# First mixer: X at the head of SyncE's load queue, branch a's convolution started earlier, its norm placed between the output projection's pieces

## The reference, cut to what matters

```
def conv_mixer(x, w_in, a_dw, a_dw_b, a_ln_g, a_ln_b, b_dw, w_out):
    u = jnp.einsum("bsd,de->bse", x, w_in)                       # 1024 -> 2560
    a_val, a_gate, b_b, b_c, b_x = jnp.split(u, [...], axis=-1)   # 512 features each
    a = a_val * jax.nn.sigmoid(a_gate)
    a = causal_depthwise_conv(a, a_dw) + a_dw_b                   # 31 taps
    a = jax.nn.silu(layer_norm(a, a_ln_g, a_ln_b))
    bb = b_b * causal_depthwise_conv(b_c * b_x, b_dw)             # 3 taps
    return jnp.einsum("bse,ed->bsd", jnp.concatenate([a, bb], axis=-1), w_out)
```

## Time and profile before

| | |
|---|---|
| median of 3 runs | 1865.94 us (1864.38 to 1869.52) |
| the profiled execution: its time | 1861.7 us |
| its span, first to last instruction | 1860.4 us |
| mean granted TensorE clock | 0.983 |
| busy TensorE matmul / weight load | 92% / 60% |
| busy VectorE / ScalarE / GpSimd | 43% / 33% / 7% |
| chain that ended last | PE 67%, DMA 21%, DVE 6%, ACT 3% |

### The profile page before, as it was taken

How to read it: one execution, slowest core, us unless ns; L and a number is a source line. 1 busy time by engine, 2 the same in 40 slices (tenths; PEclk the granted TensorE clock), 3 DMA queues, 4 the chain that set the end, 5 groups by cost and what they waited for, 6 DMA issues and landing times.

```text
span 1860.4 us, 23739 instructions
## 1 busy us (share of the span) xinstructions
PE 1710.4 (92%) x9910; PEld 1113.5 (60%) x9910; DVE 796.0 (43%) x1526; ACT 611.4 (33%) x1159; POOL 121.3 (7%) x141
## 2 busy tenths in 40 slices
PE   7978999998887987999998988699999999999998
PEld 7964443333232974344432322587999789779986
DVE  4952111111002774111110010566788667758885
ACT  4531010000001561011000001366666554646664
POOL 0000000000000000000000000033111000501110
PEclk9989999999999999999999999899999999999999
DMA  9439999999999639999999999443455544335550
GB/s 397 181 146 366 420 419 420 420 420 421 419 420 418 231 146 408 421 419 420 420 419 421 420 419 419 157 140 136 155 184 183 181 159 159 133 125 184 182 181 24
DMA packets 75362, 544.87 MB, mean 293 GB/s; under 512 B 8433, under 2 KB 8433, under 8 KB 9457
## 3 DMA queue, kind: packets, MB, share of 16 engines
q1 hardware_dynamic: 74304, 540.05, 73.0%
q10 hardware_dynamic: 944, 3.22, 0.4%
HBM read 542.19 MB, written 1.05 MB: 292 GB/s over the span
## 4 chain that ended last, share of the span: by engine, by line
PE 67%; DMA 21%; DVE 6%; ACT 3%; issue 1%; POOL 1%; SPq 0%; DVEq 0%; ACTq 0%
PE PS L897 21%; DMA ring<-in_w 16%; PE PS L342 12%; PE PS L344 12%; PE PS L343 12%; DMA F<-in_w 5%; PE PS L874 2%; PE PS L909 2%; PE PS L655 1%; DVE wl L325 1%; POOL sm L437 1%; DMA X<-in_x 1%; DVE X L547 1%; ACT wh L319 1%; PE PS L492 0%
## 5 line engine op out<-in xcount | busy, mean ns | idle before, releaser
L897 PE MATMUL PS<-ring,F 128*64 128x512 f32 x2112 | 477.7, 597 | 45.7 <-DMA ring<-in_w 41.3
L325 DVE TENSOR_TENSOR wl<-ring,wh 128x512 fp32r<-128x512 f32 x512 | 367.9, 739 | 187.2 <-ACT wh L319 184.2
L319 ACT ACTIVATE wh<-ring 128x512 fp32r<-128x512 f32 x512 | 319.4, 631 | 295.0 <-PE PS L344 291.4
L897 PEld LDWEIGHTS PS<-ring,F 128*64 128x64 f32 x2112 | 144.1, 136 | 362.7 <-issue 269.1
L342 PE MATMUL PS<-xh,wl 128*128 128x256 f32 x1216 | 351.5, 289 | 6.9 <-DVE xl L1547 2.1
L343 PE MATMUL PS<-xl,wh 128*128 128x256 f32 x1216 | 344.7, 283 | 0.0
L344 PE MATMUL PS<-xh,wh 128*128 128x256 f32 x1216 | 344.6, 283 | 0.0
L342 PEld LDWEIGHTS PS<-xh,wl 128*128 128x128 f32 x1216 | 233.9, 192 | 11.4 <-issue 5.8
L343 PEld LDWEIGHTS PS<-xl,wh 128*128 128x128 f32 x1216 | 234.1, 192 | 0.6
L344 PEld LDWEIGHTS PS<-xh,wh 128*128 128x128 f32 x1216 | 233.9, 192 | 0.0
L342 PE MATMUL PS<-wh,xl 128*128 128x512 f32 x368 | 149.0, 405 | 12.0 <-DVE wl L325 4.8
(11 more groups left out here) (332 smaller groups left out, 1746.7 us busy)
## 6 DMA issues: line engine op xcount, KB each, us to landing
ring<-in_w SPq DMA_DIRECT2D x264, 1024.0 KB, 26.5
F<-in_w SPq DMA_DIRECT2D x60, 1024.0 KB, 25.2
ring<-in_ffn_up SPq DMA_DIRECT2D x44, 1024.0 KB, 4.9
early<-in_w SPq DMA_DIRECT2D x40, 1024.0 KB, 26.2
ring<-in_ffn_down SPq DMA_DIRECT2D x22, 1024.0 KB, 4.9
ring<-in_even_w_in SPq DMA_DIRECT2D x10, 1024.0 KB, 18.3
Z<-in_w SPq DMA_DIRECT2D x10, 1024.0 KB, 24.5
XT<-in_w SPq DMA_DIRECT2D x10, 1024.0 KB, 25.3
```

What stands on the lines that cost most here:

```text
L319: act.e.activation(self.wh[:, p % NPIECE, :], self.piece_source(p), ACT.Copy).then_inc(*self.up("w_hi", p))
L325: dve.e.tensor_tensor(self.wl[:, p % NPIECE, :], self.piece_source(p), f32(self.wh[:, p % NPIECE, :]), ALU.subtract).then_inc(*self.up("w_ ...
L897: t = pe.e.matmul(PS[64 * half:64 * half + 64, bank, :], lhs(k), weights[:, a:a + 512], start=(k == 0), stop=(k == 7))
```

## The change

X is loaded by SyncE in two halves ahead of all weights; ScalarE issues its three small loads only after it has split the first four pieces. The column groups of `ew_in` come in another order: gate, value, gate, value of branch a for its first and its second half, then branch b the same way. So a's first half is ready after group 1, not after group 2. TensorE does 11 taps, 2 after each piece of groups 3 to 7 and 1 after each of group 8. VectorE starts its taps in group 2 and follows a table `steps`. In the output projection, parts 0 and 1 come first as before, but the pieces of part 0 need no wait at its start, the mean stands behind part 0, the variance after two pieces of part 1, the spread after part 1. The mean and variance go to banks 6 and 7. Scaling, affine, tanh and gate are done in halves, the tanh reads the scaled value directly (its scale and bias do the affine), the two powers become one, and part 0 gets buffers of its own (`early_gh`, `early_gl`).

```diff
-PE_TAPS = 12
+PE_TAPS = 11
-        order = {"ew_in": [2, 3, 0, 1, 6, 7, 8, 9, 4, 5], "ew_out": [2, 3, 0, 1],
+        order = {"ew_in": [2, 0, 3, 1, 6, 8, 7, 9, 4, 5], "ew_out": [2, 3, 0, 1],
+        self.left["ew_out", 0] = [nc.alloc_sbuf_tensor_at(n, [128, 2, T], F32R, offset=f_at + 4 * a)[:, :, :]
+                                  for n, a in (("early_gh", 6496), ("early_gl", 7008))]
...
-        e.dma_start(self.X[:, :, :], A["x"].rearrange("(h p) d -> p h d", p=128)).then_inc(self.s_x, 16)
+    def sync_setup(self):
+        for h in range(2):
+            self.sp.e.dma_start(self.X[:, h, :], self.A["x"][h * 128:h * 128 + 128, :]).then_inc(self.x_in[h][0], 16)
...
     def even_tensor(self):
-                for _ in range(2 if c >= 4 else 0):
+                for _ in range(0 if c < 3 or c > 8 else 1 if c == 8 else 2):
...
-        for b in range(4):
-            pe.wait_ge(self.even_bank_read(6 + b))
+        for c in (2, 3, 6, 7):
+            pe.wait_ge(self.even_bank_read(c))
         for _ in self.tensor_out("ew_out", p, 8, 0):
             pass
...
         for c in range(4):
-            pe.wait_ge(at("ev_sum", c))
-            t = pe.e.matmul(PS[:, 4, 0:256], self.mean512[:, :], v["acc"][:, c, :], start=(c == 0), stop=(c == 3))
+            pe.wait_ge(at("ev_sum", 3))
+            t = pe.e.matmul(PS[:, 6, 0:256], self.mean512[:, :], v["acc"][:, c, :], start=(c == 0), stop=(c == 3))
         t.then_inc(*up("ev_mean"))
+        for n in self.tensor_out("ew_out", p, 8, 1):
+            if n == p + 5:
+                pe.wait_ge(at("ev_square"))
...
         pe.wait_ge(at("ev_rdiag", 1), at("consts", "ones"))
...
         t.then_inc(*up("ev_spread"))
-        for _ in self.tensor_out("ew_out", p, 8, 1):
-            pass
         for _ in self.tensor_out("ew_out", p, 8, 2):
             pass
...
     def even_scalar(self):
         for n in range(NPIECE):
             self.scalar_split(n)
+        self.scalar_setup()
...
-                for _ in range(4 if (c, j) == (3, 0) else 2 if c >= 4 else 0):
...
+                for _ in range(0 if c < 2 else 2 if diag < 4 * PE_TAPS - 1 else 4 * PE_TAPS - diag):
+                    if diag >= 6:
+                        act.wait_ge(at("ev_conv", diag - 6))
...
+                if (c, j) == (9, 1):
+                    self.scalar_split_x("ew_out", 0, self.GT[:, 0:2, :], at("ev_dve", 8))
...
+        self.scalar_split_after(p)
+        self.scalar_split_x("ew_out", 1, self.GT[:, 2:4, :], at("ev_dve", 9), at("w_used", p - 1))
+        for n in range(1, 4):
             self.scalar_split_after(p + n)
         act.wait_ge(at("ev_centred"))
         act.e.activation(v["sq"], v["acc"], ACT.Square).then_inc(*up("ev_square"))
+        for n in range(4, 8):
+            self.scalar_split_after(p + n)
+        for h in range(2):
+            for c in (2 * h, 2 * h + 1):
+                act.wait_ge(at("ev_scaled", h), at("ev_var"), at("ev_consts", "bh"))
+                act.e.activation(v["sq"][:, c, :], v["acc"][:, c, :], ACT.Tanh, scale=v["gh"][:, c:c + 1],
+                                 bias=v["bh"][:, c:c + 1]).then_inc(*up("ev_tanh", c))
+            self.scalar_split_x("ew_out", 2 + h, self.GT[:, 4 + 2 * h:6 + 2 * h, :], at("ev_gated", 2 * h + 1))
...
     def even_vector(self):
+        steps = {(1, 3): [(value, 0)], (2, 0): [(convolve, 2)], (2, 1): [(convolve, 1)], (2, 2): [(convolve, 2)],
+                 (2, 3): [(convolve, 1)], (3, 3): [(convolve, 3), (value, 1)], (5, 3): [(convolve, 2), (product, 0)],
+                 (6, 3): [(convolve_b, 0)], (7, 3): [(convolve, 2), (product, 1)], (8, 2): [(convolve_b, 1)],
+                 (8, 3): [(convolve, 2), (gate_b, 0)], (9, 0): [(convolve, 2)], (9, 2): [(convolve, 1)], (9, 3): [(gate_b, 1)]}
...
+                for step, n in steps.get((c, j), [(convolve, 4 if (c, j) in ((4, 1), (5, 1), (6, 1)) else 3)] if c > 2 else []):
+                    step(n)
+        self.vector_split_x("ew_out", 1, self.GT[:, 2:4, :])
+        for n in range(2):
+            self.vector_split_after(PIECES["ew_out"] + n)
+        convolve(len(taps))
...
+        scale(0)
+        gate(0)
+        scale(1)
+        self.vector_split_x("ew_out", 2, self.GT[:, 4:6, :])
+        gate(1)
+        self.vector_split_x("ew_out", 3, self.GT[:, 6:8, :])
+        for n in range(6, 16):
             self.vector_split_after(p + n)
```

More of the change, by code:

```diff
@@ L381, in tensor_out @@
         pe, PS = self.pe, self.PS
+        xh, xl = self.operand(stage, q)
         pe.wait_ge(self.at("g_lo", stage, q))
@@ L754, in even_vector, with value @@
         dve.wait_ge(at("ev_pad"), at("ev_consts", "bh"))
+        p = PIECES["ew_in"]
         taps = [(k, c) for half in range(2) for k in range(PE_TAPS, 31) for c in (2 * half, 2 * half + 1)]
-        b_taps = [(k, c) for c in range(4) for k in range(3)]
+        def value(half):
+            c, i = 1 + 2 * half, 2 * half
+            dve.wait_ge(at("w_used", p + 4 * c + 3), at("ev_act", c - 1))
+            dve.e.scalar_tensor_tensor(out=aP[:, i:i + 2, 30:286], in0=v["sg"][:, i:i + 2, :], scalar=1.0,
+                                       in1=self.bank2(c), op0=ALU.add, op1=ALU.mult).then_inc(*up("ev_dve", c))
         def convolve(n):
@@ L769, in convolve, with product, convolve_b @@
                 t.then_inc(*up("ev_tap", c, k))
-        def convolve_b(n):
-            for _ in range(min(n, len(b_taps))):
-                k, c = b_taps.pop(0)
-                if k:
+        def product(half):
+            c, i = 5 + 2 * half, 2 * half
+            dve.wait_ge(at("w_used", p + 4 * c + 3), at("ev_act", c - 1))
+            dve.e.tensor_tensor(bP[:, i:i + 2, 2:258], v["bc"][:, i:i + 2, :], self.bank2((5, 1)[half]),
+                                ALU.mult).then_inc(*up("ev_dve", c))
+        def convolve_b(half):
+            for k in (1, 2):
+                for c in (2 * half, 2 * half + 1):
                     dve.wait_ge(at("ev_btap", c) if k == 1 else at("ev_btap2", c, 1))
@@ L801, in even_vector @@
-        p = PIECES["ew_out"]
-        for q in range(2):
-            self.vector_split_x("ew_out", q, self.GT[:, 2 * q:2 * q + 2, :])
-        for n in range(4):
-            self.vector_split_after(p + n)
-        convolve(len(taps))
+                if (c, j) == (9, 1):
+                    self.vector_split_x("ew_out", 0, self.GT[:, 0:2, :])
+                for step, n in steps.get((c, j), [(convolve, 4 if (c, j) in ((4, 1), (5, 1), (6, 1)) else 3)] if c > 2 else []):
+                    step(n)
@@ L829, in even_vector, with scale, gate @@
-        for q in (2, 3):
-            self.vector_split_x("ew_out", q, self.GT[:, 2 * q:2 * q + 2, :])
-        for n in range(4, 16):
+        for n in range(4, 6):
+            self.vector_split_after(p + n)
+        def scale(h):
+            i = 2 * h
+            dve.wait_ge(at("ev_spread"), at("ev_centred"))
+            dve.e.tensor_tensor(acc[:, i:i + 2, :], acc[:, i:i + 2, :], across.to_broadcast([128, 2, 256]),
+                                ALU.mult).then_inc(*up("ev_scaled", h))
+        def gate(h):
+            for c in (2 * h, 2 * h + 1):
+                dve.wait_ge(at("ev_scaled", h))
+                dve.e.tensor_scalar(bacc[:, c, :], acc[:, c, :], v["gh"][:, c:c + 1], v["bh"][:, c:c + 1], ALU.mult,
+                                    ALU.add).then_inc(*up("ev_affine", c))
+            for c in (2 * h, 2 * h + 1):
+                dve.wait_ge(at("ev_affine", c), at("ev_tanh", c))
+                dve.e.scalar_tensor_tensor(out=self.GT[:, 4 + c, :], in0=v["sq"][:, c, :], scalar=1.0, in1=bacc[:, c, :],
+                                           op0=ALU.add, op1=ALU.mult).then_inc(*up("ev_gated", c))
@@ L2360, in program @@
     def program(self):
[L2361 removed]
+        self.sync_setup()
         self.pool_setup()
```

140 lines of the change are left out of this document (55 added, 85 removed).

## The result

The changed kernel took 1854.49 us in the median of 6 runs (1851.21 to 1859.79), the kernel before 1868.22 in 6 runs beside it: a ratio of 0.9931, 95% interval 0.9911 to 0.995, 13 us. Over all comparisons on record the changed kernel's 23 executions have a mean of 1857.6, the 111 of the kernel before one of 1866.5: 8.9 us. The traces show 6.6 us of it at the first residual. So the first ratio was also a high draw.

The account below looks back on a forecast made before the run. In the first mixer, whose end gates the experts' weight stream, TensorE was taken as the bound up to 93.0, then the norm. Gains of 0.5 + 0.86 + 3.75 = 5.1 us took 1865.94 to 1860.8, range 1855.5 to 1866.

Parts of the forecast that it names:

- Term 1: Mixer start: X loaded first brings the first matmul 2.2 us earlier, half clock takes most back; gain 0.5 us.
- Term 3: Last projection matmul to first residual: fewer waits gain 6.55 us, lost clock behind two waits costs 2.8; gain 3.75.
- VectorE's lateness: End of the input projection: VectorE enters the mixer's end 2.5 us late, making TensorE wait 3.7 behind part 0.
- 2 us of allowance for the spread of the medians: Widening of the forecast range by 2 us, for the medians' own spread and for the waits counted.
- The path to the end: Mixer to experts: issue of weight chunk 23 gates their load stream, so all time won in the mixer counts.
- Its second part: Expert weight stream: chunk 10 is issued about 3 us earlier, the mixer ends 5 earlier, so the 3 us pause shrinks.
- Term 2: Input projection: four fewer tap matmuls on TensorE, two of them ahead of 93.0, 0.43 us each; gain 0.86 us.
- The second wait: Ahead of part 2: TensorE waits 3.6 us for scaling, tanh, gates and splits, then loses the clock, costing 1.05.
- The norm's place under part 1: Output projection: variance and spread run between pieces of part 1, which cover centring, square, power and diagonals without waits.
- Both waits shorter or without a fall of the clock: Rival, mixer's end: VectorE under 1 us late, first wait about 2.2; gain 7.4 to 8.5 us, 1857.9; chance 0.22.
- The gain is used up: Rival, start and end: start gives nothing or costs 1, clock stays low 5.6 us; gain 1.5 to 2.5; chance 0.18.
- VectorE as the bound and slower: Rival, input projection: VectorE's taps take 0.71 us instead of 0.42, TensorE waits for `wl`; 1871.5 us; chance 0.06.

Follow-up runs that it names:

- pad: Changed kernel plus 20 dummy float32 matmuls of 256 columns ahead of the mean, 8.5 us at full clock; 0.9992 of the kernel before.
- x_only: Kernel before with only X's load changed: two halves heading the load queue, small loads behind the first splits; 1.0004 of the kernel before.
- warm_start: Changed kernel plus nine dummy matmuls of 128 columns between X's transposes and the first projection matmul; 0.9954 of the kernel before.
- The three traces with the second block of dummies: Changed kernel plus eight 256-column dummy matmuls between spread and part 2: alone 0.9952, with nine more at the start 0.9933 and 0.9938 of before.
- two comparisons: The unaltered changed kernel measured twice more against the kernel before; 0.9957 and 0.9954.
- three arrangements: Changed kernel with old norm place (0.9951), part 0 split behind group 9 (0.9963), four weight splits ahead of sums (0.9966); all together 1.0008 of before.

## Why the prediction was wrong, point by point

The step that failed is the size of terms 1 and 3, with VectorE's lateness inside term 3, and 2 us of allowance for the spread of the medians; the way from the mixer to the end held.

- **The path to the end** was right: chunk 23 is the gate, it follows R and not chunk 10, and pad's 8.5 us came out as some 8 us of time. Its second part missed: chunk 10 was issued 6.0 us earlier in the means and not 3, so the pause ahead of chunk 23 did not shrink.
- **Term 1, the start (0.5 us).** The mechanism held: 3.1 us earlier at the first matmul, then half clock for 3.0, 5.2 and 5.6 us in the three traces, in the mean the 4.6 that I took. The small loads, 1.5 us in my sum, cost ScalarE nothing; its first split came 0.36 later than taken; in all the first matmul came 0.9 us earlier than forecast. At T, 2.2 us were won; less 0.86 for the two tap matmuls that are gone ahead of it, that is 1.3 us where the term had 0.5. In the time x_only showed nothing. The Trainium skill (TensorE: Matmul & The Clock Gate, Part 1) has activity alone release the throttle; warm_start agrees, with 0.39 instead of 0.58 us for the first matmul behind nine dummies and a wait of 0.96.
- **Term 2, eleven taps (0.86).** It is no gain: taps12, with the four taps back on TensorE, gives it all back as a shorter wait.
- **VectorE's lateness at T (2.5 us)** was 1.2, and the wait behind part 0 2.14 and not 3.7. I let ScalarE's one-piece delay by the diagonals last into group 8; it ended with the last diagonals, at 74.8. ScalarE's timeline of the changed kernel shows the delay itself:

```profile
32.85 0.83 ACT L720 ACTIVATE F<-ident,cols 128x128 f32<-128x128 f32 x2 [1.24 <-PE PS L668]
...
35.14 0.83 ACT L720 ACTIVATE F<-ident,cols 128x128 f32<-128x128 f32 x2 [0.45 <-PE PS L668]
```

- **Term 3 (3.75 us), the term that was mis-sized.** In three traces 38.0 - 33.6 = 4.4, in the first 5.4. The second wait was right (3.83 for 3.6), with the clock's fall behind it. Behind the first I had a fall for sure: at 2.14 us it came in two traces of three (the mean took 1.97, 3.38 and 3.20). The three traces with the second block of dummies show the parts. Counted from the end of the last projection matmul, 0.28 us behind T, the stretch takes 30.1 us with the clock kept, where I had 30.95; the long wait's fall costs 1.9 to 2.2 where I took 1.05, and the short one's 1.5 in two traces of three, 1.0 in the mean, where I took 1.75. In all 33.3 us for my 33.75. The norm's place under part 1, which the term leans on, gave 0.6 us of wait and 2.0 at R in one trace, and nothing that the time shows; no wait ahead of part 0 and the earlier sums are worth 2.6 and 2.3 at R, in one trace each.
- **Sum and range.** 5.1 us forecast, 6.6 at R in the traces, 8.9 in the means of all executions, 13 in the first comparison. Of the 1.5 us missing at R, 0.8 are term 1 and 0.7 term 3. The range failed on what I left out of it: 1854.49 is a median of 6 runs that spread over 8.6 us and lies 3.1 below the mean of the kernel's 23 executions, which is inside the range. In that comparison the median of before was also 2.3 us higher than the one I started from, which makes the first gain look larger still. Why the times differ by 2 to 3 us more than the traces show at R stays open.
- **The rivals.** "Both waits shorter or without a fall of the clock" gave 7.4 to 8.5, the number of two comparisons, but by luck: the lateness was 1.2 and the wait 2.14 as it says, yet the clock fell behind the long wait in all three traces and behind the short one in two, and R shows 6.6. "The gain is used up" did not happen. VectorE as the bound and slower: no trace has TensorE waiting for `wl` before T.

## What to carry to other kernels

Follow a chain of waits to its end before giving any one of them a price, and compare at a point of the trace, not only by the time: three arrangements, undone singly, can hardly be told from the changed kernel by their times, but show 0.6, 2.1 and 1.5 us of added wait, and nearly their sum when undone together. Work moved off the bounding engine just ahead of a wait for the engine that receives it is worth nothing: taps12 had its 1.7 us back from a wait of 2.14 that became 0.44. A long idle stretch of TensorE ahead of dense matmuls can be worth filling: eight dummy matmuls in a wait of 3.83 us made the end 1.9 to 2.2 us shorter.

## What was not expected of the hardware

Executions of the kernel before differ by up to 11.3 us (1860.50 to 1871.82 in 21), though the waits of the norm are equal to 0.01 us in its two traces. Two sources are seen in the traces. The clock is kept or lost behind the same wait: behind 1.98 us it was kept in both traces of before and lost in x_only, behind 2.14 it was kept in one of three traces of the changed kernel, and the experts' first sixteen matmuls took 3.65 us in eleven traces and 5.37 to 5.65 in six. And the code from the second mixer on, the same in all kernels, took 1251.1 to 1260.6 us; why isn't shown. ScalarE's sequencer issued three loads in the time of its first splits (8.27 to 9.62 beside work from 8.26) without delaying them.
